# A head's two score maps in the two row halves of TensorE's array, in a two-layer streaming encoder on one core

## What is computed

```
def diff_attn_prompt(q, k, v, lam):
    ...
    for i in range(T // Q_BLOCK):
        qs, qe = i * Q_BLOCK, (i + 1) * Q_BLOCK
        s = jnp.einsum('bqhcd,bkhcd->bhcqk', q[:, qs:qe], k[:, :qe]).astype(jnp.float32)
        mask = chunk_id[None, :qe] <= chunk_id[qs:qe, None]
        p = jax.nn.softmax(jnp.where(mask, s, -jnp.inf), axis=-1)
        a = (p[:, :, 0] - lam * p[:, :, 1]).astype(v.dtype)
        outs.append(jnp.einsum('bhqk,bkhv->bqhv', a, v[:, :qe]))
```

## Time and profile before

| | us |
|---|---|
| median of 3 runs | 3005.48 |
| lowest and highest | 3002.83 and 3006.07 |
| the profiled execution's own time | 3004.48 |
| its span in the profile | 3002.7 |
| TensorE busy in the span | 2876.0 (96%) |
| VectorE, ScalarE, GpSimd busy | 1212.3, 863.9, 860.4 |

### The profile page before, as it was taken

One profiled execution on the slowest core, in us unless ns is written; L12 is line 12 of the kernel. 1 busy time (PEld: TensorE's weight loads), 2 busy tenths in 40 slices (PEclk: granted clock), 3 DMA queues, 4 the chain that ended last, 5 costly groups with the idle time before them and its releaser, 6 DMA issues. The chain is left out here.

```text
span 3002.7 us, 40470 instructions
## 1 busy us (share of the span) xinstructions
PE 2876.0 (96%) x15644; PEld 2543.2 (85%) x15644; DVE 1212.3 (40%) x2185; ACT 863.9 (29%) x1738; POOL 860.4 (29%) x1067
## 2 busy tenths in 40 slices
PE   8999899999999999998999788888999999999997
PEld 8878777889988998897888678766899899989996
DVE  2256754732222222246513577743362222222226
ACT  2153241322211221122101477743241122112222
POOL 2112261521211111223212287832251111111114
PEclk9999998999999999999999899998999999999999
DMA  4111415111111111110222533285121111111101
GB/s 129 57 29 52 138 37 198 40 57 43 49 42 35 42 49 42 42 36 32 96 101 88 179 108 106 85 313 218 43 64 44 48 42 42 42 42 42 42 28 63
DMA packets 207187, 223.93 MB, mean 75 GB/s; under 512 B 42816, under 2 KB 151616, under 8 KB 207056
## 3 DMA queue, kind: packets, MB, share of 16 engines
q1 hardware_dynamic: 207056, 222.16, 22.9%
HBM read 184.90 MB, written 37.22 MB: 74 GB/s over the span
## 5 line engine op out<-in xcount | busy, mean ns | idle before, releaser
L792 POOL TENSOR_TENSOR wsplit<-raw,wsplit 128x1024 fp32r<-128x1024 f32 x192 | 459.2, 2394 | 1719.5 <-ACT wsplit L1032 1654.4
L1434 PE MATMUL ps<-xt,wsplit 128*128 128x384 f32 x5184 | 906.5, 335 | 1.4 <-DVE xt L1901 1.4
L1434 PEld LDWEIGHTS ps<-xt,wsplit 128*128 128x128 f32 x5184 | 900.9, 188 | 3.1 <-DVE xt L1901 1.8
L1625 PE MATMUL ps<-wsplit,hT 128*128 128x512 f32 x3456 | 787.8, 390 | 0.0
L1625 PEld LDWEIGHTS ps<-wsplit,hT 128*128 128x128 f32 x3456 | 649.2, 188 | 134.2
L1452 PE MATMUL ps<-wsplit,xt 128*128 128x512 f32 x2592 | 603.0, 393 | 2.8 <-DVE xt L1901 2.8
L1452 PEld LDWEIGHTS ps<-wsplit,xt 128*128 128x128 f32 x2592 | 488.2, 189 | 110.9 <-issue 6.5
L1032 ACT ACTIVATE wsplit<-raw 128x1024 fp32r<-128x1024 f32 x184 | 193.9, 1054 | 882.9 <-PE ps L1625 615.8
L2105 DVE TENSOR_TENSOR x_res<-x_res,ps 128x512 f32<-128x512 f32 x252 | 172.8, 686 | 435.0 <-PE ps L1625 435.0
L2157 DVE TENSOR_SCALAR hsq<-ps 128x384 f32<-128x384 f32 x192 | 106.9, 557 | 537.2 <-PE ps L1434 537.2
L1174 ACT ACTIVATE hsq<-hsq 128x384 f32<-128x384 f32 x192 | 101.1, 527 | 547.7 <-DVE hsq L2157 547.7
(11 more groups left out here) (186 smaller groups left out, 2382.8 us busy)
## 6 DMA issues: line engine op xcount, KB each, us to landing
raw<-in_w_up SPq DMA_DIRECT2D x64, 512.0 KB, 4.0
raw<-in_w_down SPq DMA_DIRECT2D x64, 512.0 KB, 3.6
Kc<-in_cache_k SPq DMA_DIRECT2D x8, 2048.0 KB, 9.2
Vc<-in_cache_v SPq DMA_DIRECT2D x8, 2048.0 KB, 9.5
raw<-in_w_in_a SPq DMA_DIRECT2D x24, 512.0 KB, 4.2
out<-kvs SPq DMA_DIRECT2D x36, 256.0 KB, 2.0
raw<-in_w_kv SPq DMA_DIRECT2D x16, 512.0 KB, 5.2
q_scr<-qst SPq DMA_DIRECT2D x16, 512.0 KB, 2.6
```

The costliest lines, as they stand in the source:

```text
L792: nc.gpsimd.tensor_tensor(wsplit[:, slot, 1, :], raw[:, slot, :], wsplit[:, slot, 0, :].bitcast(F32), ALU.subtract).then_inc(lo_done, 1)
L1434: last = nc.tensor.matmul(ps[0:M, b, 0:GW], st, xt[:, c, k, ng * GW:(ng + 1) * GW], start=(k == 0 and i == 0), stop=(k == KT - 1 and i == 2))
L1625: last = nc.tensor.matmul(ps[:, (v + t) % 6, :], hT[:, a, 2 * kp + k, tok:tok + P], wsplit[:, q, b, k * 512:(k + 1) * 512], start=(kp == 0 ...
```

## The change

The two maps of a head now lie in the two row halves of the array: rows 0 to 63 hold map 0, rows 64 to 127 map 1, in keys and queries alike.

- `scores(s)` makes both maps at once: for each 512 columns three passes (high by high, high by low, low by high), each as two matmuls of 64 rows, one for each map, into different banks; the mask is two matmuls of 64 rows (a second mask row is added to the constants). One signal is given for both maps.
- A head takes 6 turns instead of 8: keys once for each half, high queries, low queries. `PREPARED` tells which turn stands ahead of which step: steps i = 2 to 7 have one, i = 0 and 1 none. The first step is preceded by 3 turns instead of 4 and then 2.
- A half of the keys is loaded by one DMA instead of four; the queries of a half by two instead of one.
- Steps with i < 4 use one bank for each map, in turns (`score_banks`), so that steps i = 1 to 3 wait only for the exponentials of two steps before; the other steps wait for both exponentials of the step before.
- The order becomes: TensorE turn, scores(s+1), weights(s-1), values(s-2); VectorE both minima, remainder, copy, combine; ScalarE turn's copy, both exponentials, copy, square. GpSimd's `balance` has 3 operations instead of 5, and `factor` and `out_norm` come one step later; the exponentials wait for `balance_done` instead of `factor_done`.
- The first streams' cached keys are loaded in four pieces in heads 4 to 7 instead of one load in head 7.

```diff
@@ -411,28 +412,44 @@
         return [(0, range(4), 6 * h + i - 2), (1, range(4, i + 1), 6 * h + i - 2)]
 
     STEPS = H_B * PT
-    FIRST_PREPARED = 4
+    FIRST_PREPARED = 3
     Q_STORES = [(2 * PT - i + 2) // 3 for i in range(3)]
 
-    def prepared_at(s):
-
-        if s < 1:
-            return range(2 * s + 6, 2 * s + 8)
-        return range(s + 7, min(s + 8, 8 * H_B))
+    def turned_before(i):
+
+        return 0 if i < 3 else i - 2 if i < 12 else 8 * (i // 6 - 1) + 2 + i % 6
+
+    PREPARED = [[i for i in range(3, 6 * H_B) if turned_before(i) == s] for s in range(STEPS)]
 
     def turn(i):
 
-        h, j = i // 8, i % 8
-        return h, ("k", "q")[j // 2 % 2], j % 2, j // 4
+        h, j = i // 6, i % 6
+        return h, ("k", "q", "q")[j % 3], j % 3 - 1, j // 3
 
     def turned(i):
 
-        h, mat, c, part = turn(i)
-        return (keys_split if mat == "k" else queries_in, 4 * h + 2 * part + c + 1)
+        h, mat, part_of, half = turn(i)
+        if mat == "k":
+            return keys_split, 2 * h + half + 1
+        return queries_in, 4 * h + 2 * half + part_of + 1
 
     def p_bank(i):
 
-        return 4 + i % 4 if i < 8 else 4
+        return 4 + i if i < 3 else 4
+
+    def last_of_pair(i):
+
+        h, half, mat = i // 4, i % 4 // 2, i % 2
+        return 6 * h + 3 * half + 2 * mat - 3 if mat == 0 else 6 * h + 3 * half - 1
+
+    def score_banks(s, c):
+
+        return (2 * c + s % 2,) if s % PT < 4 else (2 * c, 2 * c + 1)
+
+    def score_cols(s, c):
+
+        banks, w = score_banks(s, c), (s % PT + 1) * P
+        return ps[:, banks[0]:banks[-1] + 1, :].rearrange("p a n -> p (a n)")[:, 0:w]
 
     def after_norm(lay):
...
@@ -640,22 +657,22 @@
             h, mat, part = i // 4, i % 2, i % 4 // 2
             if i >= 2:
 
-                sp.wait_ge(turned_full, 2 * i - 2)
+                sp.wait_ge(turned_full, last_of_pair(i) + 1)
             if mat == 0:
-                src = k_prompt[0].rearrange("(t p) h c d -> p t h c d", p=P)[:, 4 * part:4 * part + 4, h]
-                for dup in range(2):
-                    for c in range(2):
-                        sp.dma_start(kqd[:, 0, :, c, dup, :], src[:, :, c]).then_inc(pair_loaded[0], 16)
+                src = k_prompt[0].rearrange("(t p) h c d -> p t h (c d)", p=P)[:, 4 * part:4 * part + 4, h]
+                sp.dma_start(kqd[:, 0], src).then_inc(pair_loaded[0], 16)
             else:
-                src = q_scr[4 * part:4 * part + 4, :, 2 * h:2 * h + 2].rearrange("t p c s d -> p t (c s d)")
-                sp.dma_start(kqd[:, 1].rearrange("p t c s d -> p t (c s d)"), src).then_inc(pair_loaded[1], 16)
+                for s in range(2):
+                    src = q_scr[4 * part:4 * part + 4, :, s, h * P:(h + 1) * P].rearrange("t p n -> p t n")
+                    sp.dma_start(kqd[:, 1 + s], src).then_inc(pair_loaded[1], 16)
 
         def kv_store(u, t):
             n = u * TILES + t
...
@@ -715,8 +734,9 @@
             sp.dma_start(Vc[:, b % 2], cache_v[b].rearrange("(t p) h v -> p t (h v)", p=P)).then_inc(vc_in[b % 2], 16)
 
         for s in range(STEPS):
-            if s % 2 == 0 and 6 + s // 2 < 4 * H_B:
-                pair_in(6 + s // 2)
+            for i in range(6, 4 * H_B):
+                if turned_before(last_of_pair(i)) - 3 == s:
+                    pair_in(i)
...
@@ -724,11 +744,10 @@
                 sp.wait_ge(lo_done, G_O2 + 4)
                 for i, src in enumerate((kv_dst[0][PT], qs_scr)):
                     sp.dma_start(kqS[:, i, :], src).then_inc(smp_qk_in, 16)
-            if s == STEPS - PT:
-
-                sp.wait_ge(turned_full, 8 * H_B)
-                sp.wait_ge(s_full, 2 * (STEPS - PT))
-                keys_in(0)
+            if s in (4 * PT, 5 * PT, 6 * PT, 7 * PT):
+
+                kt = s // PT - 4
+                sp.dma_start(Kc[:, 0, kt], cache_k[0, kt * P:(kt + 1) * P].rearrange("p h c d -> p (h c d)")).then_inc(kc_in[0], 16)
             out_o(s)
 
...
@@ -939,10 +958,8 @@
             r = s % 4
             pool.wait_ge(exp_done, 2 * s + 2)
             small(tt, rl[:, r, 1:2], ls[:, r, 1:2], neg1[:, 0:1], ALU.pow)
-            small(tt, gf[:, r:r + 1], ls[:, r, 0:1], rl[:, r, 1:2], ALU.mult)
-            small(tt, gf[:, r:r + 1], gf[:, r:r + 1], nlam, ALU.mult, done=balance_done)
-            small(tt, rq[:, r:r + 1], ls[:, r, 0:1], ls[:, r, 0:1], ALU.mult)
-            small(ts, rq[:, r:r + 1], rq[:, r:r + 1], EPS, None, ALU.mult)
+            small(ts, gf[:, r:r + 1], ls[:, r, 0:1], rl[:, r, 1:2], nlam, ALU.mult, ALU.mult, done=balance_done)
+            small(ts, rq[:, r:r + 1], ls[:, r, 0:1], ls[:, r, 0:1], EPS, ALU.mult, ALU.mult)
 
         def factor(s):
...
@@ -960,12 +977,12 @@
                                     ALU.mult).then_inc(out_normed, 1)
 
         pool.wait_ge(lambda_done, 1)
-        for s in range(STEPS + 2):
+        for s in range(STEPS + 3):
             if s < STEPS:
                 balance(s)
-            if s >= 2:
-                factor(s - 2)
-                out_norm(s - 2)
+            if s >= 3:
+                factor(s - 3)
+                out_norm(s - 3)
             if 2 <= s < 6:
...
@@ -1299,8 +1316,8 @@
 
                 bank, _, use = a_banks(s - 4)[-1]
                 act.wait_ge(a_full[bank], use + 1)
-                act.wait_ge(factor_done, s - 3)
-            nc.scalar.activation(PR[:, s % 4, c, 0:w], ps[:, 2 * c:2 * c + 2, :].rearrange("p a n -> p (a n)")[:, 0:w],
+                act.wait_ge(balance_done, s - 2)
+            nc.scalar.activation(PR[:, s % 4, c, 0:w], score_cols(s, c),
                                  ACT.Exp, bias=mx[:, s % 2, c:c + 1], scale=-1.0,
                                  accum_out=ls[:, s % 4, c:c + 1]).then_inc(exp_done, 1)
...
@@ -1330,14 +1347,13 @@
         for i in range(FIRST_PREPARED):
             prepare(i)
         for s in range(-1, STEPS + 2):
-            for i in prepared_at(s):
-                prepare(i)
             if s + 1 < STEPS:
+                for i in PREPARED[s + 1]:
+                    prepare(i)
                 exponentials(s + 1, 0)
+                exponentials(s + 1, 1)
             if 0 <= s - 1 < STEPS:
                 weights_out(s - 1)
-            if s + 1 < STEPS:
-                exponentials(s + 1, 1)
             if 0 <= s - 2:
                 out_square(s - 2)
...
@@ -1726,38 +1742,39 @@
         def prepare(i):
 
 
-            h, mat, c, part = turn(i)
-            if c == 0:
-                n = 2 * h + part + 1
-                pe.wait_ge(pair_loaded[mat == "q"], 64 * n if mat == "k" else 16 * n)
-            if i == 8:
-                pe.wait_ge(keys_split, 4)
-                pe.wait_ge(queries_in, 4)
-            elif i >= 4:
-                pe.wait_ge(*turned(i - 1 if i > 8 else i - 4))
+            h, mat, part_of, half = turn(i)
+            if mat == "k":
+                pe.wait_ge(pair_loaded[0], 16 * (2 * h + half + 1))
+            elif part_of == 0:
+                pe.wait_ge(pair_loaded[1], 32 * (2 * h + half + 1))
+            if i >= FIRST_PREPARED:
+                pe.wait_ge(*turned(i - 1 if i > FIRST_PREPARED else 0))
             for k in range(4):
-                last = nc.tensor.transpose(ps[:, p_bank(i), k * P:(k + 1) * P],
-                                           kqd[:, int(mat == "q"), k, c].rearrange("p a d -> p (a d)"), ident)
+                last = nc.tensor.transpose(ps[:, p_bank(i), k * P:(k + 1) * P], kqd[:, part_of + 1, k, :], ident)
             last.then_inc(turned_full, 1)
 
-        def scores(s, c):
+        def scores(s):
+
+
             h, i = s // PT, s % PT
             w = (i + 1) * P
             if i in (0, 4):
-
-                pe.wait_ge(keys_split, 4 * h + (2 if i == 0 else 4))
+                pe.wait_ge(keys_split, 2 * h + (1 if i == 0 else 2))
                 pe.wait_ge(queries_in, 4 * h + (2 if i == 0 else 4))
             if s:
-                pe.wait_ge(exp_done, 2 * (s - 1) + c + 1)
+                pe.wait_ge(exp_done, 2 * s - 2 if 1 <= i < 4 else 2 * s)
+            rows = [slice(c * HD, (c + 1) * HD) for c in range(2)]
             for b in range((w + 511) // 512):
                 n = min(512, w - 512 * b)
-                o = ps[:, 2 * c + b, 0:n]
-                q = QS[:, h % 2, c, i * P:(i + 1) * P]
-                nc.tensor.matmul(o, q, KD[:, h % 2, 0, c, 512 * b:512 * b + n], start=True, stop=False)
-                nc.tensor.matmul(o, q, KD[:, h % 2, 1, c, 512 * b:512 * b + n], start=False, stop=True)
-
-            nc.tensor.matmul(ps[:, 2 * c + b, n - P:n], mrow[:, 0:P], mrow[:, P:2 * P],
-                             start=False, stop=True, skip_group_check=True).then_inc(s_full, 1)
+                for q, k in PASSES:
+                    for c in range(2):
+                        nc.tensor.matmul(ps[:, score_banks(s, c)[b], 0:n], QS[rows[c], h % 2, q, i * P:(i + 1) * P],
+                                         KD[rows[c], h % 2, k, 512 * b:512 * b + n],
```

(27 more changed lines are left out.)

41 lines of the change are left out of this document (22 added, 19 removed).

## The result

The changed kernel takes 3013.13 us (median of 8 runs, 3011.8 to 3014.0 when one disturbed run is left out) against 3005.78 for the kernel before in the same job: 1.0025 times as long, 95% interval 1.0014 to 1.0036. The forecast was 3004, inside the bound of 0.2%; the time lies outside that bound, on the slow side, and inside the range of 2995 to 3020. The profiled execution took 3012.43 us, with a span of 3010.6.

The account below looks back on a forecast made before the run. The prediction took the six middle heads to be bound by TensorE's own work, with short waits. Start -5.2, first head -3.2 and six heads +7.0 gave -1.4 us, a median of 3004, range 2995 to 3020.

Parts of the forecast that it names:

- the clock's term in the sum: TensorE's clock: the sum added 1.0 us for it in the first head and nothing in the middle and last heads.
- rival 5: Middle heads: TensorE's clock falls to 1.2 GHz for a tenth of the stage, +8 us, 3012; chance 0.08.
- The six heads: Six middle heads: 31.97 us each against 30.81, 1.16 more a head, 7.0 more in all.
- Scores up to the mask: Both maps' score products per step, paired side by side: 0.48 us at i = 0 up to 1.50 at i = 7.
- the strips: Sample streams' attention: products in four column strips ran side by side, taken as nearest evidence that row-half pairs cost one pitch.
- Rivals 2 and 3: Score pairs: a pair's weight loads queue, 3019, chance 0.11; or products do not pair at all, 3057, chance 0.07.
- the 0.1 of the sum: Steps i = 0, 1, 2: 0.1 us each for TensorE's change of array shape.
- The ring: Wide steps: scores wait for both previous exponentials; scores, two minima, second exponential and 0.42 hand-overs, 3.29 to 5.47 us.
- The start: Stage start up to step 1's scores: one DMA for the late keys lets them begin 5.2 us sooner.
- first head: Rest of the first head: 32.2 us against 35.40, 3.2 less, with 1.0 added for the clock.
- The last head: Last head with its tail: left unchanged, losing 1.2 us in the ring, gaining from both maps' last scores being ready together.
- Rival 4: Query loads issued late, so their turns come late: every head waits 1.3 us, +9, 3013; chance 0.14.

Follow-up runs that it names:

- e2: Changed kernel plus unread TensorE products behind i = 7's weight products and at steps i = 3, 4 and 6, where TensorE waits: 3004.61 us.
- e1: Changed kernel plus 12 unread TensorE products of 256 columns behind the last query step's (i = 7) weight products: 3007.72 us.
- e7: Changed kernel with both maps' products in the first row half of the array, map 1's scores computed from map 0's queries and keys: 3109.56 us.
- e8: Kernel before with GpSimd's part of the change alone (shorter balance, factor and norm one step later, exponentials waiting for the balance): 2979.21 us.
- e6: Changed kernel with the two maps' scores apart at i = 0 and 4 to 7, each waiting for its own map's exponential: 3000.40 us.
- e15: As e6, with each pair of query loads placed one step sooner in SyncE's queue: 2993.56 us.
- e5: Kernel before with turns 4 to 7 of the first head moved behind step 0's scores: 3006.65 us.

## Why the prediction failed

- **The step that failed** is the clock's term in the sum: the middle heads and the last one were taken at full clock, and rival 5, a falling clock, had a chance of 0.08. The changed kernel loses 8.5 us to the clock (e2), and without it the median is 3004.61 against the 3004 forecast. Rival 5 was argued from busy shares, a fall at 25.82 of 35.40 us and none at 32.14 of 43.36, which settle nothing. It did not look at the one new thing on TensorE, a standstill of 1.5 us or more at every head's end, longer than any of the waits in the earlier trace rows. Its price of 8 us met the measured 8.5 by luck: it came from scores that run slowly in the ring steps, and what runs slowly in the middle heads is step 0, TensorE's own work, which follows the longest wait.
- **The six heads** were forecast 7.0 longer and are 14.0 longer: 5.2 of the difference is the clock (e1), and 1.7 is the first of them, where a fourth turn (0.5) stands ahead of the narrow steps and a query load comes 1 us late. The sum had neither.
- **That e2 lands on the 3004** is luck in part. Its stage against the earlier trace rows is 4.2 shorter at the start (forecast 5.2), 2.7 in the first head (3.2), 8.7 longer in the six heads (7.0) and 1.6 shorter in the last (0 forecast): together 0.1 longer where the forecast had 1.4 shorter, and the stages ahead happened to end 1.4 sooner in its profiled execution.
- **Scores up to the mask**: forecast 1.50 at i = 7, measured 1.50; the strips were the right row. Rivals 2 and 3 are refuted: six products of 128 columns up to their mask take 0.36 in pairs and 0.70 in one row half (e7), both at full clock. The Trainium skill's rule that loads overlap where row groups differ (TensorE: Matmul & The Clock Gate, Part 3) is borne out by that. Its warning of a drain (TensorEngine Tiling (Array Packing), Key Properties) can cost little here. The full-array transposes start 0.15 after the masks (1822.87 and 1823.02), 0.07 after one mask before; and the 64-row scores start 0.53 after a turn does (1800.82 and 1801.35), 0.35 in the full array, a difference that also holds the first product's exposed load. That is near the 0.1 of the sum.
- **The ring**: forecast 3.29, 4.02, 4.42, 4.96, 5.47 for i = 3 to 7; measured 3.39, 3.96, 4.56, 4.86, 5.50. A head without a fall is 31.97 forecast, 31.99 measured. At i = 5 what TensorE waits for is not the second exponential but its turn, which waits 1.35 us for VectorE's remainder of the keys; that may be the 0.14 by which this step is longer than forecast. One link is not told apart by the records: the second exponential starts at 1825.52, when the first (to 1825.50) and the second minimum (to 1825.49) have both just ended. For i = 0 to 2 the terms that the prediction names add up to 2.80, 3.53 and 3.08 where it says 2.93, 3.66 and 3.22; some 0.13 a step stands in the figures without a term, and with it they are near the measured 2.85, 3.64 and 3.26.
- **The start** was forecast 5.2 shorter and is 4.4; the **first head** 3.2 and is 2.7 at clock 0.73. The 1.0 that the sum added there for the clock is not seen: with clock 0.89 (e1, e2) the first head takes 32.6 and 32.7, as it does at 0.73. When the stage begins scatters from run to run: the first scores of the kernels with the changed start lie between 1688.7 and 1693.7, so the 2.05 us by which this stage began sooner is not counted.
- **The last head** was left as it is and costs 2.3. At full clock (e2) it takes 41.8, which is 1.6 less than before, and 3.9 of clock (0.85 in the window) turn it over. That the 1.6 come from both maps' last scores being ready together was argued in the prediction, and no run tries it.
- **A reading that did no harm to the sum, but was wrong**: "the six heads are TensorE's own work, with short waits". The 18.6 us of waits in the earlier trace rows were GpSimd's queue, and the part of the change that I named only for the first head shortens the six heads by 17 us (184.87 to 167.80, e8) when nothing else is changed. The ring then adds 4.0 a head to 27.97, and the clock the rest. That is where the change's gain went: one part of it is worth 26.6 us alone, and the rest of the change (the pairs with their ring and their falls, the new turns and loads) gives it all back and 7 more.
- **Rival 4** held in small: the query loads come late, at 1 us in the second head, and are hidden by the ring in the others until it is shortened (e6, e15).

## What to carry to other kernels

Pairing the scores of two softmaxes shortens their products (2.0 to 1.50 us in the widest step) and makes both ready at once, and with that takes away the work that ran beside the first one's minimum and exponential; before saving work on an engine, ask what filled its waits. A short wait for another engine's result can hide an in-order queue: look at what stands ahead of the awaited instruction there, and move a wait for a late result behind the work that others wait for. Where a forecast contains a new wait of one to two microseconds on TensorE, price a fall of its clock behind it as a term of the sum, with a chance: here it came behind four of six such waits, and cost 8.5 us in all. And before two stage profiles are compared, take off the time by which the stage itself began sooner or later; e5's 3.2 us were mostly that.

## What the runs showed of the hardware that was not expected

- After a wait of 1.86 us at the end of a head, TensorE's clock fell for part of the next step in four of six heads, and not in the other two; with the wait filled down to 0.44 (e1) it stayed at 1.00 in all. One fall cost 1.0 to 1.6 us in step 0 and 1.5 to 1.7 in its head. Waits of 1.3 us in the same heads had no fall behind them, and in e7 the clock stood at 1.2 GHz for 20 us of nearly unbroken work: in these runs the length of one wait does not decide it.
- Two products in different row halves run side by side even with three products of the busy half between them in the queue (twelve in 1.49 us); with six, the first product of the other half starts beside the third, with three still to come, and only part is paired (2.08); in one half, not at all (3.00).
- GpSimd's one-column operations stretch at times: the reciprocal that mostly takes 0.57 us took 1.57 in this record of e8_before_pool, while VectorE combined 1024 columns:

```profile
1819.76 1.28 DVE L2365 SCALAR_TENSOR_TENSOR PR<-PR,stats 128x1024 f32<-128x1024 f32 x1
1819.88 1.57 POOL L928 TENSOR_TENSOR stats<-stats,cst 128x1 f32<-128x1 f32 x1
```
